# Twelve products of the constant ones ahead of TensorE's first operands, and the first weight columns loaded and split as pieces of their own

## The reference

```
h = _rmsnorm(x, norm_gain) @ w_in
u, z_a, q, k, v, z_b, g_a, g_b = jnp.split(h, SPLITS, axis=-1)
```

## Time and profile before

| | us |
|---|---|
| median of 3 runs | 1551.42 (1551.1 to 1551.95) |
| the profiled execution, its own time | 1548.85 |
| its span in the profile | 1547.1 |
| PE busy in it | 1530.3 (99%) |
| DVE busy | 656.6 (42%) |
| ACT busy | 423.5 (27%) |
| POOL busy | 485.1 (31%) |

### The profile page before, as it was taken

One profiled execution on the slowest core, in us unless ns is written; L12 is line 12 of the kernel. 1 busy time (PEld: TensorE's weight loads), 2 busy tenths in 40 slices (PEclk: granted clock), 3 DMA queues, 4 the chain that ended last, 5 costly groups with the idle time before them and its releaser, 6 DMA issues.

```text
span 1547.1 us, 22408 instructions
## 1 busy us (share of the span) xinstructions
PE 1530.3 (99%) x8861; PEld 1321.7 (85%) x8861; DVE 656.6 (42%) x1032; ACT 423.5 (27%) x576; POOL 485.1 (31%) x117
## 2 busy tenths in 40 slices
PE   7999999999999999999999999999999999999998
PEld 7989888999999978777787887779988888888887
DVE  7798871238786142433425233347512233500000
ACT  7302232421111313333232332334501112311110
POOL 4233232323233232232322322233333333333331
PEclk9999999999999999999999999999999999999999
DMA  7525449743223454455545455446324324342440
GB/s 276 139 72 166 133 143 178 224 146 116 98 107 110 131 145 107 124 150 140 126 122 140 120 134 147 131 170 226 130 101 150 129 76 150 116 149 75 132 147 35
DMA packets 166635, 209.26 MB, mean 135 GB/s; under 512 B 106640, under 2 KB 124848, under 8 KB 152880
## 3 DMA queue, kind: packets, MB, share of 16 engines
q1 hardware_dynamic: 63840, 133.85, 28.5%
q10 hardware_dynamic: 102736, 74.57, 16.2%
HBM read 162.99 MB, written 42.76 MB: 133 GB/s over the span
## 4 chain that ended last, share of the span: by engine, by line
PE 94%; DVE 4%; issue 1%; DMA 1%; SPq 0%; ACT 0%; ACTq 0%; DVEq 0%
PE ps L782 34%; PE ps L473 21%; PE ps L877 14%; PE ps L570 9%; PE ps L785 8%; PE ps L694 1%; PE ps L717 1%; PE ps L703 1%; DVE pt L1411 1%; PE ps L677 1%; DVE ssum L1392 1%; PE ps L743 1%; DMA x_raw<-in_xT 1%; PE ps L551 1%; PE ps L711 0%
## 5 line engine op out<-in xcount | busy, mean ns | idle before, releaser
L440 POOL TENSOR_TENSOR w_lo<-raw,w_hi 128x2048 fp32r<-128x2048 f32 (+1 forms) x111 | 484.5, 4367 | 1036.8 <-ACT w_hi L910 1036.8
L910 ACT ACTIVATE w_hi<-raw 128x2048 fp32r<-128x2048 f32 (+1 forms) x111 | 197.2, 1777 | 674.4 <-PE ps L785 278.4
L782 PE MATMUL ps<-x_hi,w_hi 128*128 128x512 f32 x512 | 205.6, 402 | 0.0
L782 PE MATMUL ps<-x_hi,w_lo 128*128 128x512 f32 x512 | 199.8, 390 | 0.0
L782 PE MATMUL ps<-x_lo,w_hi 128*128 128x512 f32 x512 | 199.7, 390 | 0.0
L473 PE MATMUL ps<-x_hi,w_hi 128*128 128x320 f32 x768 | 176.7, 312 | 12.1 <-DVE x_lo L1400 8.2
L473 PE MATMUL ps<-x_lo,w_hi 128*128 128x320 f32 x768 | 175.7, 310 | 0.0
L473 PE MATMUL ps<-x_hi,w_lo 128*128 128x320 f32 x768 | 175.6, 310 | 0.0
L473 PEld LDWEIGHTS ps<-x_hi,w_hi 128*128 128x128 f32 x768 | 128.8, 189 | 13.3 <-POOL w_lo L440 8.5
L473 PEld LDWEIGHTS ps<-x_lo,w_hi 128*128 128x128 f32 x768 | 129.0, 189 | 0.0
L473 PEld LDWEIGHTS ps<-x_hi,w_lo 128*128 128x128 f32 x768 | 129.0, 188 | 0.0
(11 more groups left out here) (254 smaller groups left out, 2434.4 us busy)
## 6 DMA issues: line engine op xcount, KB each, us to landing
raw<-in_wts SPq DMA_DIRECT2D x99, 1024.0 KB, 5.0
g_scr<-gbuf ACTq DMA_DIRECT2D x8, 1024.0 KB, 8.1
gate_in<-g_scr ACTq DMA_DIRECT2D x8, 1024.0 KB, 6.2
x_raw<-in_xT SPq DMA_DIRECT2D x16, 320.0 KB, 7.8
z_scr<-E ACTq DMA_DIRECT2D x16, 320.0 KB, 2.2
Y<-in_x_tok ACTq DMA_DIRECT2D x20, 256.0 KB, 4.6
out_y_tok<-Y ACTq DMA_DIRECT2D x20, 256.0 KB, 2.9
c_scr<-powers SPq DMA_DIRECT2D x16, 256.0 KB, 4.2
```

Source lines behind the costliest of these rows:

```text
L440: return nc.gpsimd.tensor_tensor(w_lo[p][:, cols], raw[p][:, cols], w_hi[p][:, cols].bitcast(F32), ALU.subtract)
L782: last = nc.tensor.matmul(ps[:, bank, :], w[p][:, col + P * i:col + P * i + P], act[:, 0:PROMPT], start=opens, stop=final and w is w_lo)
L910: return nc.scalar.activation(out, in_, func, **kw)
```

## The change

PE executes twelve products of `ones` with itself (128 x 128, float32) into PSUM bank 7 before its first real operand; it waits only for POOL's first memset (`prep`). The first quarter of both weight units is cut in two pieces: 128 columns (K tile 0) and 384 columns (K tiles 1 to 3). SP loads the two small pieces, then x tile 0, then the two large pieces, then x tiles 1 to 3; the large pieces and x tile 1 increment one semaphore, for which ACT waits once (48). ACT and POOL split in the same pieces. The counts of `part_hi` and `part_split` that others wait for are two higher.

```diff
-            for q in range(4):
+            for p in range(2):
+                spe.dma_start(raw[p][:, 0:P], wts[p][:, 0:P]).then_inc(part_loaded[p], 16)
+            spe.dma_start(x_raw[:, 0, :], xT[0]).then_inc(x_loaded[0], 16)
+            for p in range(2):
+                spe.dma_start(raw[p][:, P:4 * P], wts[p][:, P:4 * P]).then_inc(x_loaded[1], 16)
+            for k in range(1, 4):
+                spe.dma_start(x_raw[:, k, :], xT[k]).then_inc(x_loaded[k], 16)
+            for q in range(1, 4):
...
-                    spe.wait_ge(part_split, 2 * q + 1)
+                    spe.wait_ge(part_split, 2 * q + 3)
...
             pool.wait_ge(prep, 2)
-            for q in range(4):
+            for p in range(2):
+                pool.wait_ge(part_hi, p + 1)
+                low(p, slice(0, P)).then_inc(part_split, 1)
+            for p in range(2):
+                pool.wait_ge(part_hi, p + 3)
+                low(p, slice(P, 4 * P)).then_inc(part_split, 1)
+            for q in range(1, 4):
...
+            pe.wait_ge(prep, 1)
+            for i in range(WARM):
+                nc.tensor.matmul(ps[:, 7, 0:P], ones[:], ones[:], start=True, stop=True)
             for k in range(KT):
                 for p in range(2):
-                    if k in (0, 4, 8):
-                        pe.wait_ge(part_split, 2 * (k // 4) + p + 1)
+                    if k < 2:
+                        pe.wait_ge(part_split, 2 * k + p + 1)
+                    if k in (4, 8):
+                        pe.wait_ge(part_split, 2 * (k // 4) + p + 3)
...
             for k in range(KT):
-                if k % 4 == 0:
+                if k == 0:
+                    for p in range(2):
+                        act.wait_ge(part_loaded[p], 16)
+                        A(w_hi[p][:, 0:P], raw[p][:, 0:P], ACT.Copy).then_inc(part_hi, 1)
+                elif k == 1:
+                    act.wait_ge(x_loaded[1], 48)
+                    for p in range(2):
+                        A(w_hi[p][:, P:4 * P], raw[p][:, P:4 * P], ACT.Copy).then_inc(part_hi, 1)
+                elif k % 4 == 0:
...
-                act.wait_ge(x_loaded[k], 16)
+                if k != 1:
+                    act.wait_ge(x_loaded[k], 16)
```

More of the change, by code:

```diff
@@ L60 @@
 SQ_LAG = 8
+WARM = 12
 SSM_BANK = (6, 7, 5, 6)
@@ L443, in _ @@
             pool.wait_ge(prep, 2)
-            for q in range(4):
+            for p in range(2):
[5 more added lines that the diff above has]
+            for q in range(1, 4):
                 for p in range(2):
                     if q < 3:
-                        pool.wait_ge(part_hi, 2 * q + p + 1)
+                        pool.wait_ge(part_hi, 2 * q + p + 3)
                     else:
@@ L452, in _ @@
                 if q < 3:
-                    pool.wait_ge(part_hi, 6 + q + 1)
+                    pool.wait_ge(part_hi, 8 + q + 1)
                 else:
@@ L502, in parts_of_unit2 @@
                 if k in (0, 4, 8):
-                    pe.wait_ge(part_split, 6 + k // 4 + 1)
+                    pe.wait_ge(part_split, 8 + k // 4 + 1)
                 if k == 12:
```

## The result

| | before | after |
|---|---|---|
| median of all runs on one chip, us | 1550.43 (22 runs, 1549.05 to 1551.95) | 1552.63 (22 runs, 1550.0 to 1554.71) |
| ratio to before, 95% interval | | 1.0014 [1.0008, 1.0020] |
| the profiled execution's span, us | 1547.1 | 1549.9 |

The interval lies above 1, so the changed kernel is slower, by 1.2 to 3.1 us, and this is within the 0.2% that the prediction called no change. The forecast was +0.2 us; the ratio says about +2.2.

What follows compares the result with a forecast made beforehand. The prediction took the load-ACT-DVE chain from x tile 8 to unit 2 at 38.46 us as the bound. PE's gain became waiting; the load added 0.2 us to 1551.42, giving 1551.6 us, range 1549.5 to 1553.0.

Steps and rivals of the forecast that it cites:

- its own signs: Prediction wrong if unit 2 starts before 38 us, or x_hi of tile 8 starts outside 16.1 to 17.3.
- What bounds the kernel now: Up to unit 2 at 38.46 us, the chain runs from x tile 8's load over ACT and DVE, not PE's work.
- PE's start, earlier by 1.5 us: At the first operand: x_hi of tile 0 at 4.8 us, PE beginning at 6.7 instead of 8.18.
- The twelve products: Ahead of PE's first operand: done at about 6.1 us, so PE meets it warm or nearly so.
- The new wait at K tile 1: PE gets K tile 1 at about 10 us (10.7 if POOL delays DVE), idling from 8.5.
- What becomes of the 1.7 us: PE ends unit 1 at 36.5 us, then waits for ACT's copy; the gain at unit 2 is nothing.
- What does move the chain: the load: x tile 8's load, first microseconds: 0.2 us later; ends -0.2 and +0.91.
- Only the bytes count: At x tile 8's load: the queue keeps DMA engines full, so two more issues (0.91 us) do not delay landing.
- catches up: ACT, with two more instructions and the combined wait, is 0.3 us late at x_hi(4) and regains it by K tile 8.
- POOL's four smaller splits: They lie ahead of 10 us, where DVE has only x_lo(1) to lose.
- The load comes late: Rival, chance 0.10: issues or combined wait delay ACT up to K tile 8, by up to 0.91 us, 1552.3.
- A lock that falls the other way: Rival, chance 0.04: near 57.9 us DVE's product starts before POOL's split, PE's 3.7 us waits go, 1547.7.

Runs made afterwards that it cites:

- the first four experiments: Kernel before plus twelve products, 1551.0 us; changed kernel without products, 1552.31; changed kernel with old loads, 1551.43; kernel before with only the new load list, 1550.77.
- larger pieces: Kernel before with only SP's load list changed, each first weight quarter loaded as two pieces of 256 columns, 128 KB each: 1551.84 us, ratio 1.0007.

## Why the prediction was right, and where it was wrong

The time fell in the range and in the forecast's case, no change within 0.2%; 1552.63 is 1.0 us over the predicted 1551.6. But of the difference the prediction gave 0.2 us and 2.2 were measured. That the time came so near is in part luck: the prediction started from 1551.42, the median of three runs, where 22 runs of the same kernel gave 1550.43, and this 1.0 us hid half of the miss. By its own signs the prediction was wrong: x_hi of tile 8 at 18.11, outside 16.1 to 17.3, unit 2 at 40.36 for 38.5 to 38.8, and a wait of 0.74 us for `u_raw` for 1.9.

- *What bounds the kernel now*: right. The chain kept its links, and with the products alone PE's gain turned into a wait of 1.63 us ahead of unit 2, with no change in the time.
- *PE's start, earlier by 1.5 us*: 6.71, predicted 6.7. x_hi of tile 0 began at 4.82 for 4.8.
- *The twelve products*: done at 5.89 for 6.1, PE warm.
- *The new wait at K tile 1*: it ended at 11.44, predicted 10 to 10.7, since the load was late (8.06 for 7.1) and POOL's split, from 8.67 on, lay beside x_lo of tile 1. That the idle time would take the clock away again, from 11.8 to 15.4, was not foreseen. It cost nothing at unit 2: PE still waited 0.74 us there.
- *What becomes of the 1.7 us*: right in that nothing reached unit 2, but there were no 1.7 us left to lose. The wait of 2.74 us and the pairs at half the clock took more than the early start gave. PE ended unit 1 at 39.62, where the prediction had 36.5 and the kernel before 38.2 to 38.4.
- *What does move the chain: the load.* This is the term that was mis-sized: taken 0.2, ends -0.2 to +0.91, measured 1.79 at x_hi of tile 8 and 1.90 at unit 2. Two sentences of it failed. "Only the bytes count" took a queue at a share of 1.03 for one whose rate is given. The new list alone cost 0.79 there, at an equal number of bytes. And "catches up", for ACT, failed too: with the splits in pieces and the old loads x_hi of tile 8 was 0.58 late, of which ACT had 0.52 from a late x tile 0 and could not make it up. The two sum to 1.37, and that is what the pieces without the products show (17.69). The changed kernel has 0.42 more, with the 0.74 us wait at 16.65 and 366 GB/s from 12 to 16 us, where its twin without the products moved 408. Whether the products or chance made that is not settled. It did not count: unit 2 began at 40.36 and 40.34.
- *POOL's four smaller splits* have "only x_lo(1) to lose": wrong for the splits alone, where the later quarters of POOL moved onto DVE's x_lo. In the changed kernel the sums follow x_hi of tile 8 by 30.1 us, as before (30.0), so there this term was nothing.
- The Trainium skill (Perfetto Trace Analysis, DMA Optimizations) says that larger DMAs use the memory's bandwidth better and that small ones, under 2 KB, carry an overhead. The prediction set this aside for the two queues' mean time of a packet. The runs agree with the direction: 241 to 253 GB/s with a DMA of 64 to 160 KB among the first, 280 to 289 without. They show it far above the page's 2 KB, and with rows of 2560 bytes too. Means over a span of 1547 us could not show what a dozen DMAs do in the first 12 us.
- *The load comes late* (0.10) is the rival that came true, at twice its price (1.79 to 1.90 for 0.91). *A lock that falls the other way* did not: POOL's split began at 59.72 and DVE's product at 59.82, a margin of 0.10 for 0.09, and the product took 5.22 us.
- The 1.54 us behind 104 us stand in the profile of after and in those of the splits alone, of two more and of two fewer DMAs, and the same seven or so pairs at 0.53 us in those of the products alone (from 102.9) and of the pieces alone (from 106.8), but not in that of before. The profiled execution of two fewer DMAs took 1551.38 us, its median is 1549.68. Executions of one kernel differ in the same way: of 33 of the kernel before, taken beside the first four experiments, the 14 with a mean granted clock of 1.000 have a median of 1549.9 us and the 7 with 0.998 one of 1551.15. So I take it for chance, which adds to the scatter. All 22 runs of after had 0.998 or 0.999; how much of its 2.2 us comes from more frequent stretches at half the clock was not separated.

## What to carry to other kernels

A wait at the start is worth shortening only up to the point where another chain meets it: here 1.5 us less at the first matmul brought nothing, and neither did a warm clock as long as ACT's copies stood behind squares that waited for DVE. With the copies moved, and with enough products to reach up to the first operand, the kernel got faster. Products that end too early are lost: with the splits alone and with the copies earlier the clock had fallen by the first operand, and in the changed kernel it fell behind the first K tile. Do not pay for an early first tile with small DMAs in front of a load that a chain hangs on; look at GB/s in short windows, not at the busy share, which was 0.81 and 0.79 up to 12 us.

## What the hardware showed that was not expected

- A few small DMAs among the first loads take 11 to 15% of the rate up to 12 us (241 to 253 GB/s for 284), with the same bytes, whether their rows have 512, 1024 or 2560 bytes, and whether there are two DMAs more or none more. Between 5 and 6 us the engines are 0.90 busy at 170 GB/s where they were 1.01 busy at 366. The kernel with x tile 0 first also dips there (207 GB/s), but had moved more ahead of it.
- A wait of 2.74 us behind 12 fast matmuls dropped the granted clock to 0.50 for about 3.6 us. Waits between the products and the first operand did so too at 2.65 and 2.72 us, and not at 1.65 and 1.90. One of 1.94 us ahead of unit 2 did so with the pieces alone and not with larger pieces. One of 2.2 us near 104 did so in some profiles (96 matmuls in 15.85 us) and not in others (14.31). No limit is to be read from these rows; they overlap.
- A cold start is not a fixed cost: PE took 6 to 10 pairs at 0.53 us from its first operand before the pace changed, in kernels that had given it nothing to do until then. The column of the granted clock reads 1.00 there.
- DVE's x_lo takes 0.87 us alone and mostly 1.83 to 1.97 with a split of POOL beside it (1.0 to 1.7 in some places), in every kernel; cutting POOL's splits only chooses which of them meet.
